# At the borders between projections and Strassen pairs of a feed-forward block: what VectorE, ScalarE and GpSimd do, in which order, and who makes the low parts of every second hidden tile

## The reference, cut to what matters

```python
def conv_ffn(h, w_up, conv_w, w_down, buf):
    u, new_buf = causal_dwconv(h @ w_up, buf, conv_w)
    a, g = jnp.split(u, 2, axis=-1)
    return (jax.nn.silu(a) * g) @ w_down, new_buf
...
        yp, bp = conv_ffn(rmsnorm(xp, norm_ffn[l]), ffn_up[l], ffn_conv[l], ffn_down[l],
                          jnp.zeros((b, CONV_W - 1, 2 * D_FF), xp.dtype))
        xp = xp + yp
```

## Time and profile before

| | |
|---|---|
| median of 3 runs | 2903.4 us (2901.64 to 2904.61) |
| the profiled execution: its own time | 2907.81 us |
| its span, first to last instruction | 2906.0 us |
| mean granted TensorE clock | 0.96 |
| PE (matmul) busy | 2643.3 us, 91% of the span |
| DVE (VectorE) busy | 1687.4 us, 58% |
| ACT (ScalarE) busy | 1195.0 us, 41% |
| POOL (GpSimd) busy | 679.3 us, 23% |
| layer 0's FFN | 1112 to 1808 us of the span |
| layer 1's FFN | 2189 us to the end |

### The profile page before, as it was taken

The page is one execution under the profiler, slowest core; times in us unless marked ns, Lnnn a source line. Parts: engine busy times, 40 slices in busy tenths (PEclk is TensorE's granted clock), DMA queues, the critical chain, the costliest instruction groups (busy, mean ns, idle before and its releaser), DMA issues.

```text
span 2906.0 us, 47440 instructions
## 1 busy us (share of the span) xinstructions
PE 2643.3 (91%) x18583; PEld 1866.0 (64%) x18583; DVE 1687.4 (58%) x2621; ACT 1195.0 (41%) x1753; POOL 679.3 (23%) x735
## 2 busy tenths in 40 slices
PE   5898998898887798999999998999989999999987
PEld 2766676655565565676677667566655676677665
DVE  8254454326899737575664666522346675665566
ACT  4665664322777624433432433211124333432432
POOL 0321303313444200222321331011101232332231
PEclk9898999999999799999999999999999999999998
DMA  3222223364000211111111111111111111111112
GB/s 131 80 72 62 66 67 121 99 185 123 1 1 1 81 51 37 49 41 63 51 44 59 51 36 64 44 51 51 51 37 44 47 62 44 51 51 48 54 42 81
DMA packets 118130, 173.69 MB, mean 60 GB/s; under 512 B 17505, under 2 KB 86482, under 8 KB 117586
## 3 DMA queue, kind: packets, MB, share of 16 engines
q1 hardware_dynamic: 97218, 150.90, 16.3%
q0 software_dynamic: 3792, 12.58, 1.3%
q10 hardware_dynamic: 16960, 8.16, 1.0%
HBM read 161.47 MB, written 14.30 MB: 60 GB/s over the span
## 4 chain that ended last, share of the span: by engine, by line
PE 71%; DVE 16%; ACT 5%; issue 3%; SPq 3%; DMA 1%; POOL 0%; ACTq 0%; DVEq 0%; POOLq 0%
PE PS L2097 48%; PE PS L2542 12%; ACT xT L1006 2%; DVE R L1745 2%; SPq L667 2%; PE PS L2130 2%; SPq L670 2%; DVE R L1415 2%; DVE R L1724 1%; PE PS L2198 1%; DVE R L1409 1%; DVE hT L1420 1%; PE PS L2365 1%; DVE R L1898 1%; PE PS L2296 1%
## 5 line engine op out<-in xcount | busy, mean ns | idle before, releaser
L2097 PE MATMUL PS<-hT,R 128*128 128x344 f16 x10152 | 1486.9, 310 | 9.7 <-DVE R L643 4.5
L2097 PEld LDWEIGHTS PS<-hT,R 128*128 128x128 f16 x10152 | 992.2, 98 | 501.5 <-issue 7.9
L643 DVE SCALAR_TENSOR_TENSOR R<-W,R 128x1024 f16<-128x1024 f32 x158 | 229.1, 1450 | 571.8 <-ACT R L637 571.1
L637 ACT ACTIVATE R<-W 128x1024 f16<-128x1024 f32 x158 | 166.3, 1053 | 650.0 <-PE PS L2097 637.7
L2542 PE MATMUL PS<-R 128*128 128x258 f16 x3360 | 386.4, 278 | 33.9 <-ACT R L1294 18.4
L2542 PEld LDWEIGHTS PS<-R 128*128 128x128 f16 x3360 | 330.9, 99 | 88.8 <-ACT R L1294 20.1
L913 POOL TENSOR_TENSOR R<-R 128x1548 f16<-128x1548 f32 (+2 forms) x88 | 198.6, 2270 | 269.3 <-ACT R L1347 269.3
L904 POOL COPY R<-R 128x2 f32<-128x2 f32 x88 | 42.9, 488 | 688.8 <-ACT R L1333 688.8
L1867 DVE SCALAR_TENSOR_TENSOR R<-R 128x1024 f32<-128x1024 f32 x96 | 137.6, 1434 | 50.4 <-ACT R L1334 49.1
L1347 ACT ACTIVATE R<-R 128x1548 f16<-128x1548 f32 (+2 forms) x88 | 84.9, 990 | 196.4 <-DVE R L2005 130.4
L1916 DVE SCALAR_TENSOR_TENSOR xT<-PS,xT 128x516 f32<-128x516 f32 x132 | 91.3, 693 | 119.7 <-PE PS L2542 108.7
(11 more groups left out here) (318 smaller groups left out, 3344.2 us busy)
## 6 DMA issues: line engine op xcount, KB each, us to landing
W<-wk SPq DMA_DIRECT2D x154, 512.0 KB, 3.5
xT<-cmp_t SPq DMA_DIRECT2D x256, 64.0 KB, 1.8
xT<-x SPq DMA_DIRECT2D x16, 516.0 KB, 7.1
W<-wdn SPq DMA_DIRECT2D x16, 512.0 KB, 3.6
W<-wdn SPq DMA_DIRECT2D x16, 384.0 KB, 3.2
W<-wdn SPq DMA_DIRECT2D x16, 320.0 KB, 2.9
o_y<-hT SPq DMA_DIRECT2D x6, 688.0 KB, 3.4
o_win_s<-state_win POOLq DMA_DIRECT2D x1, 4088.0 KB, 24.0
```

The lines of the kernel that those rows point to most:

```text
L637: act.activation(to[:, n, 0, :], W[:, n, :], ACT.Copy, scale=UNIT).then_inc(wh_here, 1)
L643: dve.scalar_tensor_tensor(to[:, n, 1, :], W[:, n, :], UNIT, to[:, n, 0, :], ALU.mult, ALU.subtract).then_inc(w_split, 1)
L2097: ins = pe.matmul(wide(u)[:, m, :], weights[half], src[:, other, m * TW:(m + 1) * TW], start=(first and half == other == 0), stop=(last an ...
```

## The change

1. GpSimd keeps the low part of turn 0 only; those of turns 1 to 3 go to VectorE (`odd_hidden`, `low_part`), between the sums. VectorE now waits there for ScalarE's high parts.
2. At the two inner borders the seven weight blocks of the first pair are split during the last but one up tile (12 and 28), and the taps, the silu and the gate of the last one (13 and 29, `BORDER`) are done within the first pair: behind the copy to `E1` on ScalarE, behind read 1 on VectorE.
3. Before tile 6 the sums and blocks 0 to 4 of pair (2,0) are made during up tile 42, blocks 5 and 6 behind tile 43's hidden sums.
4. The first two up tiles behind a part's pairs are written out; the first waits for five reads only, the second for six. The order of TensorE's work stays the same.

```diff
+BORDER = (13, 29)
...
                     for k, cols in hidden_spans(h):
+                        if k:
+                            continue
                         pool.wait_ge(zhi_here, 4 * (layer * KH + h // 2) + k + 1)
...
+            def hidden_high(layer, h):
+                act.wait_ge(y_here, layer * KF + h + 1)
+                act.activation(Y[0], Y[0], ACT.Silu).then_inc(silu_here, 1)
+                for turn, cols in hidden_spans(h):
+                    act.wait_ge(zm_here, layer * KF + h + 1)
+                    if turn >= 2:
+                        act.wait_ge(t4_here, 2 * (layer * KH + h // 2) + turn - 1)
+                    raw, to = cols
+                    act.activation(ZC[:, z_slot(h), 0, to], ZR[:, raw], ACT.Copy).then_inc(zhi_here, 1)
...
                 act.activation(two(E1), accumulator(part, 0), ACT.Copy, scale=1 / UNIT).then_inc(e1_here, 1)
+                if part < 2 and j == 0:
+                    hidden_high(layer, BORDER[part] // 2)
...
-                    if after[0] == "tile":
-                        blocks_high(layer, second, range(1))
...
-                    if after[0] == "pair":
-                        blocks_high(layer, after, range(3, BLOCKS))
-                    if n == 0:
+                    if after[0] == "up" and second[0] == "pair":
+                        blocks_high(layer, second, range(3, BLOCKS))
+                    if second[0] == "tile":
+                        blocks_high(layer, FFN[at_item + 3], range(5))
+                    if n == 0 or after[0] == "pair":
                         continue
...
+                    hidden_high(layer, h)
                     if after[0] == "tile":
-                        blocks_high(layer, second, range(1, BLOCKS))
+                        blocks_high(layer, second, range(5, BLOCKS))
...
                 dve.wait_ge(e1_added, 3 * s + 1)
                 read(1, t, 1, 1)
+                if part < 2 and j == 0:
+                    k = BORDER[part]
+                    taps(Y[1], U[1], lambda r: FS[:, k, r, :], lambda r: FW[:, k, r:r + 1])
+                    gated(layer, k // 2)
...
+            def odd_hidden(layer, h):
+                (_, odd), (_, most), (_, rest) = hidden_spans(h)[-3:]
+                dve.wait_ge(zm_here, layer * KF + h + 1)
+                hidden_sum(0)
+                hidden_sum(1)
+                dve.wait_ge(z_here, 4 * (layer * KH + h // 2) + 1)
+                low_part(layer, h, 1, odd)
+                hidden_sum(2, t4_here)
+                hidden_sum(3, t4_here)
+                low_part(layer, h, 2, most)
+                low_part(layer, h, 3, rest)
...
+            def low_part(layer, h, turn, cols):
+                raw, to = cols
+                z = ZC[:, z_slot(h), :, to]
+                dve.wait_ge(zhi_here, 4 * (layer * KH + h // 2) + turn + 1)
+                dve.tensor_tensor(z[:, 1], ZR[:, raw], z[:, 0], ALU.subtract).then_inc(z_here, 1)
...
                     dve.wait_ge(u_here, tiles + k + 1)
+                    if after[0] == "pair":
+                        continue
                     taps(Y[n], U[n], lambda r: FS[:, k, r, :], lambda r: FW[:, k, r:r + 1], None if n else y_here)
-                    if after[0] == "pair":
-                        blocks_low(layer, after, range(3, BLOCKS))
-                    if after[0] == "tile":
-                        sums(layer, second, range(2))
+                    if after[0] == "up" and second[0] == "pair":
+                        blocks_low(layer, second, range(3, BLOCKS))
+                    if second[0] == "tile":
+                        first = FFN[at_item + 3]
+                        sums(layer, first, range(3))
+                        blocks_low(layer, first, range(3))
+                        sums(layer, first, range(3, 4))
+                        blocks_low(layer, first, range(3, 5))
...
                     if h % 2:
-                        dve.wait_ge(zm_here, layer * KF + h + 1)
-                        hidden_sums(layer, h)
+                        odd_hidden(layer, h)
                     if after[0] == "tile":
-                        sums(layer, second, range(2, 3))
-                        blocks_low(layer, second, range(1, 3))
-                        sums(layer, second, range(3, 4))
-                        blocks_low(layer, second, range(3, BLOCKS))
+                        blocks_low(layer, second, range(5, BLOCKS))
...
                 for part, (start, stop) in enumerate(((0, 14), (14, 30), (30, 44))):
+                    start = max(start, 2)
                     if part:
-                        pe.wait_ge(product_read, 6 * (PAIR[layer, ("pair", part - 1, 3)] + 1))
-                    start = max(start, 2)
+                        for k in range(2):
+                            pe.wait_ge(product_read, 6 * PAIR[layer, ("pair", part - 1, 3)] + 5 + k)
+                            up(start + k, STEP[layer, ("up", start + k)])
+                        start += 2
```

More of the change, by code:

```diff
@@ L1952, in pair_turn, with turned, hidden_sum, gated @@
                     blocks_low(layer, after, range(6, 7))
[L1954 to L1959, removed]
-                dve.tensor_tensor(t4, b21, t2, ALU.subtract).then_inc(t4_here, 1)
-                if h >= FIRST[2]:
-                    dve.wait_ge(z_here, 4 * (layer * KH + h // 2) + 1)
-                dve.tensor_tensor(b12, b22, b12, ALU.subtract).then_inc(t4_here, 1)
+            def turned(n):
+                return ZR[:, n * HT:(n + 1) * HT]
+            def hidden_sum(n, done=None):
+                to, one, other = ((4, 1, 0), (5, 3, 4), (6, 2, 5), (1, 3, 1))[n]
+                ins = dve.tensor_tensor(turned(to), turned(one), turned(other), ALU.subtract)
+                if done is None:
+                    own.link(ins)
+                else:
+                    ins.then_inc(done, 1)
+            def odd_hidden(layer, h):
[9 more added lines that the diff above has]
+                low_part(layer, h, 3, rest)
+            def gated(layer, h):
+                dve.wait_ge(silu_here, layer * KF + h + 1)
+                if h % 2 == 0:
+                    dve.wait_ge(z_here, 4 * (layer * KH + h // 2))
+                dve.tensor_tensor(ZR[:, (h % 2) * TT:(h % 2 + 1) * TT], Y[0], Y[1], ALU.mult).then_inc(zm_here, 1)
+            def low_part(layer, h, turn, cols):
[3 more added lines that the diff above has]
+                dve.tensor_tensor(z[:, 1], ZR[:, raw], z[:, 0], ALU.subtract).then_inc(z_here, 1)
             def ffn(layer, norm, last=False):
@@ L1989, in ffn @@
                         sums(layer, second, range(3, 4))
[L1990 to L1991 removed]
                     wait_emptied(dve, u + k)
                     dve.wait_ge(u_here, tiles + k + 1)
+                    if after[0] == "pair":
+                        continue
                     taps(Y[n], U[n], lambda r: FS[:, k, r, :], lambda r: FW[:, k, r:r + 1], None if n else y_here)
[L1995 to L1998 removed]
+                    if after[0] == "up" and second[0] == "pair":
[6 more added lines that the diff above has]
+                        blocks_low(layer, first, range(3, 5))
                     if n == 0:
                         continue
[L2001 to L2006 removed]
+                    gated(layer, h)
                     if h % 2:
[L2008 to L2009 removed]
+                        odd_hidden(layer, h)
                     if after[0] == "tile":
[L2011 to L2014 removed]
+                        blocks_low(layer, second, range(5, BLOCKS))
                 v = PLAN[f"down{layer}"][0] + 1
```

16 lines of the change are left out of this document (removed).

## The result

The changed kernel's median is 2882.3 us (four runs, 2876.7 to 2883.5) beside 2902.5 for the kernel before (four runs, 2899.4 to 2904.6): a ratio of 0.9927, 95% interval 0.9910 to 0.9945. It is 20.2 us faster, where 32.4 were forecast. The profiled execution's span is 2881.8 us, 24.2 less than before; its own time is 2883.5.

A forecast was written before the change was run, and what follows sets the result against it. TensorE, 91% of the span, bounds the kernel; only its waits in the FFN can shrink. Gains of 16.8 (layer 0) and 15.6 (layer 1) make 32.4: 2907.8 becomes 2875.4, less 4.4 to the median, 2871.0 us; range 2862 to 2887.

The forecast's parts named there:

- E1's wait gone, product 5's in its place: First pairs, layer 0: inner E1 waits of 4.84 and 4.06 us go; product 5 waits 4.0, 2.1 and, last border, 1.9.
- Restarts, tile 6: Behind a part's pairs two waits of 1.06 us go, 2.1 a layer; tile 6's 2.43 us wait at the last border goes.
- Contention of the moved taps: First border, behind read 1: GpSimd's additions until 1262.7 add about 0.9 us to 4.25 us of taps and gate.
- The clock behind the new waits: Lower clock behind product 5's waits at the three borders costs 1.5, 0.7 and 0.7 us a layer.
- The last border's wait on the reload: Pair (2,0): seventh block done at 1732.4, product 5 wanted at 1742.1 and resumed at 1744.0, a wait of 1.9 us.
- VectorE's busy time: Sign to look for in the profile: VectorE's busy time up by some 30 to 50 us, GpSimd's down by over 100.
- dear inner borders: Rival: new waits at the inner borders cost what the old did, leaving restarts and last border; 2880.5 us, chance 0.14.
- low parts as dear as on GpSimd: Rival: VectorE's low parts take 6.5 us instead of 3.7, 2.8 later at every border; 2886 us, chance 0.10.
- The rival of no clock loss: Rival: the new waits are too short to lower the clock, 5.8 us more gain; 2865.2 us, chance 0.12.
- the slower case: Rival: VectorE falls behind in the projections, TensorE stands at 20 odd hidden tiles, 40 us back; 2911 us, chance 0.04.

The follow-up runs named there:

- Experiment 4: The changed kernel with silu of tiles 13 and 29 ahead of the copy to E1, their taps and gate ahead of read 1 again: 2883.7 us.
- experiment 3: The changed kernel, but the first up tile behind a part's pairs waits for the sixth read again: 2880.1 us.
- experiment 5: The changed kernel with taps of tiles 13 and 29 behind the first pair's last low part, the gate behind the second pair's: 2866.9 us.
- experiment 7: The changed kernel with the edits of experiment 5 and Experiment 6 together: 2853.7 us, ratio 0.9835 to the kernel before.
- experiment 9: The changed kernel run and profiled once more, with no edit: 2876.7 us, ratio 0.9918 to the kernel before.
- Experiment 6: The changed kernel with all seven weight blocks of pair (2,0) split during tile 42: 2869.2 us.
- experiment 8: The kernel of experiment 7 with the low parts of turns 1 to 3 back on GpSimd: 2860.0 us.

## Why the prediction was right, and where it was too high

The direction, the places and the mechanisms held; the time, 2882.3, is inside the range and 11.3 above the forecast. By its own steps:

- **E1's wait gone, product 5's in its place:** right at the inner borders, 4.0 and 2.1 us forecast, 3.98 and 2.39 measured; too small at the last, 1.9 forecast, 3.64 and 2.78 measured (below). The working of the first border came out to 0.3 us: read 3 was put at 1270.0 and ended at 1269.7. Some of that is luck: the taps and the gate took 5.3 us, not 5.15, and the seven operations behind them 3.7, not 4.1. Experiment 4 shows that the two halves of that step are separate: with the early weight blocks E1's wait is gone without the deferral, which is worth 3.7 us beside them.
- **Restarts, tile 6:** right. All four restarts went, worth 4.0 us by experiment 3, 4.2 forecast.
- **Contention of the moved taps:** I took 0.9 us, less than the whole 1.9 that the Trainium skill's rule would give (SBUF — State Buffer, Who interferes with whom). VectorE's timeline of the changed kernel:

```profile
1260.67 1.50 DVE L1877 SCALAR_TENSOR_TENSOR R<-R 128x1024 f32<-128x1024 f32 x1
1262.10 1.24 DVE L1878 SCALAR_TENSOR_TENSOR R<-R 128x8 f32<-128x8 f32 x1
1263.38 1.28 DVE L1879 SCALAR_TENSOR_TENSOR R<-R 128x1024 f32<-128x1024 f32 x1
```

  1.50 and 1.24 where 1.28 and 0.22 are clean: 1.2 us. GpSimd's three additions ran until 1263.3, 2.6 us beyond read 1, and VectorE lost less than half of that. The rule's lock agrees with the short operation, more than five times as long; that VectorE would stand until the additions end does not agree, and the rows at hand bounded the sum better.
- **The clock behind the new waits: the step that failed most.** The prediction took 1.5, 0.7 and 0.7 us a layer, 5.8 in all. Clean lengths are in experiments 5 and 7: 12.11 us for 108 matmuls, 61.10 for 552, and 42.57 for 384 (experiment 5's chain). Against these the changed kernel's chain shows 2.4, 1.7 and 2.7 in layer 0, 1.7, 1.7 and 1.5 in layer 1: 11.7, so 5.9 more. In its second profile (experiment 9) they are 2.6, 1.7 and 1.5, then 1.5, 1.7 and 0.0: 9.0, so 3.2 more. The granted clock by stretch:

```profile
1268.00:1272.00 4.00, 2.21 (x11) 1.57 (x12) 4.00 (x9) 1.39 (x4) 0.00 (x0) 0.50 0.00 0
1272.00:1276.00 4.00, 4.00 (x26) 3.02 (x25) 1.37 (x3) 0.52 (x1) 0.00 (x0) 0.66 0.00 0
1504.00:1508.00 4.00, 4.00 (x26) 3.01 (x24) 2.44 (x5) 0.63 (x1) 0.00 (x0) 0.65 0.00 0
1740.00:1744.00 4.00, 3.84 (x18) 2.69 (x19) 3.11 (x6) 0.00 (x0) 0.00 (x0) 0.50 0.02 4
```

  Behind each of the three waits it is at the lower level, 1.2 GHz, for some microseconds with TensorE never idle again. Before, the last border's 384 matmuls took 44.16 behind 3.56 us, which I knew and cut to 0.7 because the wait would be shorter; it wasn't.
- **The last border's wait on the reload, 1.9 forecast, 0.41 + 3.64 measured in layer 0 and 0.41 + 2.78 in layer 1.** The working took the low parts of blocks 5 and 6 at 0.65 us each. VectorE's timeline:

```profile
1725.67 2.37 DVE L1908 SCALAR_TENSOR_TENSOR R<-W,R 128x512 f16<-128x512 f32 x2
...
1734.53 0.69 DVE L1901 TENSOR_TENSOR HM<-W 128x512 f32<-128x512 f32 x1 [3.54 <-DMA W<-wdn]
```

  They took 2.37, just as in the earlier trace rows, and for the same reason: GpSimd's addition of `E1` begins at 1726.06, and one of them lasts 1.77 us where 0.68 is clean. So the slots come free 16.0 us behind tile 43's end, not 14.9, and the reload took 6.5 us from there in layer 0, not 5.9 to 6.4. Those 6.5 are the exception: it took 5.6 in layer 1, and 5.7 and 5.5 in experiment 9. With the usual reload the waits are 2.7 to 2.8 us, and the slow one makes the rest of the 3.64; why it was slow is open. The low parts' row stood in front of me. Experiment 6 confirms the chain: with both blocks made earlier the wait is gone.
- **VectorE's busy time "up by some 30 to 50" was wrong:** it fell by 26. In layer 0's first projections:

```profile
L644 DVE SCALAR_TENSOR_TENSOR R<-W,R 128x1024 f16<-128x1024 f32 x13 | 15.9, 1225 | 45.0 <-ACT R L638 45.0
L1976 DVE TENSOR_TENSOR R<-R 128x516 f32<-128x516 f32 x12 | 8.1, 691 | 0.2
L2009 DVE TENSOR_TENSOR R<-R 128x1548 f16<-128x1548 f32 x3 | 5.3, 1770 | 3.0 <-ACT R L1300 3.0
```

  The low part of 1,548 columns is 1.77 us as forecast (1.8), the hidden sum 0.69 instead of 2.52. But the weight split too had been stretched by GpSimd (1,465 ns before the change, 1,225 now), and the first tap (1,422 and 1,284), which the prediction left out.

Add up: the clock 5.9 and the last border's waits 2.2 and 1.3 make 9.4; less 0.7 gained in the projections, which the forecast left out, and 0.4 elsewhere, they are the 8.3 us between 32.4 and the profile's 24.1. Against the second profile the gap is 4.7. The other 4 us of the result are no part of the mechanism: the profiled execution before stood 5.3 us above the median of its runs, that of the changed kernel 1.2. Of the rivals, "dear inner borders" and "low parts as dear as on GpSimd" gave 2880.5 and 2886, near the measured time by accident: the inner borders did gain, in layer 1 and at the second one, and the low parts cost what was forecast. The rival of no clock loss had the sign of the error wrong, and TensorE never waits inside the projections, against the slower case.

## What to carry to other kernels

When work is deferred past a wait, list in order which reads stand behind it on that engine: here the taps and the gate only passed the wait from product 2 to product 5, and paid off (15.5 us more) once they stood behind the last read that TensorE wants. Price the wait that takes another's place with the clock loss of the waits that the trace already shows, not with less because it should be shorter. And price a moved operation by its row at the place where it will run: a neighbour's operation on GpSimd makes the same shape 0.7 or 1.8 us. To price an edit from single profiles, compare only the part that it touches, and profile one kernel twice first to see what repeats: whole FFNs differed by 3.6 us with nothing changed.

## What the runs showed of the hardware, not expected

- The loss of clock behind one and the same wait differs between executions: 384 matmuls of the last border took 45.29 us behind 3.64 (changed kernel, layer 0), 44.11 behind 2.78 (layer 1), 44.12 behind 2.81 and 42.58 behind 2.67 in experiment 9, and in experiment 5's two layers 42.57 behind 2.79 and 44.05 behind 2.72. Waits of 0.88 and 1.08 us cost nothing in experiment 7 (108 matmuls in 12.11 us, 552 in 61.10), nor did one of 1.91 in experiment 8 (552 in 61.11), while behind 2.39 or 2.40 the same 552 took 62.77 in both layers of both profiles of the changed kernel.
- A VectorE operation on eight columns took 1.24 us beside GpSimd's addition and 0.22 alone. In experiment 4's rows the three taps that meet GpSimd's additions are longer by 1.03, 0.97 and 1.01 us, two of them on 8 columns and one on 1,024; in the changed kernel one on 1,024 columns is longer by only 0.22. So the size of an operation did not decide what it lost. That the number of operations does is a guess from these few.
- What lies ahead of the FFN, where no instruction was changed, varies between executions: layer 0's up tiles start at 1114.6 us in experiment 7's profile and at 1122.1 in experiment 8's. Differences of a few us between kernels are therefore read from the stretch that the edit touches.
